# From routing to the first expert: two gathers issued inside the routing's part, levels taken last, four idle transposes in place of 24, x's low parts between two weights' low parts

## The reference, cut to what matters

```python
def hierarchical_moe(u, wg, bg, we, be, w_gate, w_up, w_down):
    xt = u.reshape(t, d)
    g_probs = softmax(xt @ wg + bg);  g_p, g_idx = lax.top_k(g_probs, 1)
    e_in_group = take_along_axis((xt @ we + be).reshape(t, 4, 8), g_idx)
    top_l, top_i = lax.top_k(e_in_group, 2)          # two experts for each token
    gates = g_p * softmax(top_l)
    ...                                              # tokens sorted by expert, in blocks of 128
    x_buf = xt[tok_buf]                              # gather of each block's rows
    def expert_block(args):
        xb, e = args
        return (silu(xb @ w_gate[e]) * (xb @ w_up[e])) @ w_down[e]
    ...                                              # rows scattered back, weighted by the gates
```

## Time and profile before

| | us |
|---|---|
| median of three executions | 2121.59 |
| the profiled execution | 2121.26 |
| its span, first to last instruction | 2119.6 |
| TensorE busy in the span | 2048.2 (97%) |
| VectorE busy | 1605.7 (76%) |
| ScalarE busy | 1361.3 (64%) |
| GpSimd busy | 258.4 (12%) |

### The profile page before, as it was taken

The page is one execution under the profiler, slowest core; times in us unless marked ns, Lnnn a source line. Parts: engine busy times, 40 slices in busy tenths (PEclk is TensorE's granted clock), DMA queues, the critical chain, the costliest instruction groups (busy, mean ns, idle before and its releaser), DMA issues. The chain is left out here.

```text
span 2119.6 us, 30221 instructions
## 1 busy us (share of the span) xinstructions
PE 2048.2 (97%) x10536; PEld 1661.8 (78%) x10536; DVE 1605.7 (76%) x2000; ACT 1361.3 (64%) x1794; POOL 258.4 (12%) x334
## 2 busy tenths in 40 slices
PE   8999998998999999999999989999899999999998
PEld 6888877777788888888877866767688888888885
DVE  4551246777888888888886266887898888888886
ACT  5333426562778787878773256765578888777784
POOL 2000000001111111111102320110111111112210
PEclk9999999999999999999999999999999999999999
DMA  4112222215999999999984020011699999999996
GB/s 138 40 60 90 78 77 74 81 61 196 339 383 388 388 387 384 379 380 380 386 313 144 1 90 11 21 60 50 241 374 380 381 386 386 385 389 384 385 364 253
DMA packets 123491, 513.28 MB, mean 242 GB/s; under 512 B 27373, under 2 KB 28490, under 8 KB 89610
## 3 DMA queue, kind: packets, MB, share of 16 engines
q1 hardware_dynamic: 103674, 474.11, 59.5%
q0 software_dynamic: 18576, 33.86, 4.2%
q10 hardware_dynamic: 1152, 4.19, 0.5%
HBM read 495.05 MB, written 50.86 MB: 258 GB/s over the span
## 5 line engine op out<-in xcount | busy, mean ns | idle before, releaser
L542 DVE TENSOR_TENSOR exp_w_lo<-ring_raw,first_w_hi 128x2048 fp32r<-128x2048 f32 x192 | 439.0, 2288 | 35.2 <-ACT first_w_hi L469 35.2
L542 DVE TENSOR_TENSOR exp_w_lo<-ring_raw,exp_w_hi 128x2048 fp32r<-128x2048 f32 x192 | 439.1, 2289 | 29.8 <-ACT exp_w_hi L469 29.8
L469 ACT ACTIVATE exp_w_hi<-ring_raw 128x2048 fp32r<-128x2048 f32 x192 | 367.8, 1918 | 61.1 <-PE exp_up_out L394 31.1
L469 ACT ACTIVATE first_w_hi<-ring_raw 128x2048 fp32r<-128x2048 f32 x188 | 360.7, 1919 | 60.6 <-PE exp_up_out L394 28.7
L394 PE MATMUL exp_gate_out<-exp_w_lo,exp_x_hi 128*128 128x512 f32 x512 | 200.9, 392 | 0.0
L394 PE MATMUL exp_y_out<-exp_w_lo,exp_hid_hi 128*128 128x512 f32 x512 | 200.2, 391 | 0.0
L394 PE MATMUL exp_up_out<-exp_w_lo,exp_x_hi 128*128 128x512 f32 x512 | 199.2, 389 | 0.0
L339 POOL DMA_INDIRECT y_rows<-exp_y,base_rows_y x63 | 75.6, 1200 | 955.2 <-ACT exp_y L489 955.2
L394 PE MATMUL exp_gate_out<-first_w_hi,exp_x_hi 128*128 128x512 f32 x272 | 109.8, 404 | 3.1 <-issue 2.0
L394 PEld LDWEIGHTS exp_gate_out<-exp_w_lo,exp_x_hi 128*128 128x128 f32 x512 | 96.7, 189 | 19.2 <-issue 0.2
L394 PEld LDWEIGHTS exp_up_out<-exp_w_lo,exp_x_hi 128*128 128x128 f32 x512 | 96.1, 188 | 19.9
(11 more groups left out here) (529 smaller groups left out, 4700.2 us busy)
## 6 DMA issues: line engine op xcount, KB each, us to landing
ring_raw<-in_expert_w_gate_dram SPq DMA_DIRECT2D x128, 1024.0 KB, 10.5
ring_raw<-in_expert_w_up_dram SPq DMA_DIRECT2D x128, 1024.0 KB, 10.9
ring_raw<-in_expert_w_down_dram SPq DMA_DIRECT2D x128, 1024.0 KB, 10.9
l0w_raw<-in_ab_w_in_dram SPq DMA_DIRECT2D x48, 256.0 KB, 2.8
finish_y<-y_rows SPq DMA_DIRECT2D x8, 1024.0 KB, 12.3
ring_raw<-in_swa_w_qkv_dram SPq DMA_DIRECT2D x5, 1024.0 KB, 10.3
ring_raw<-y_rows SPq DMA_DIRECT2D x10, 512.0 KB, 5.1
base_h<-in_x_dram ACTq DMA_DIRECT2D x8, 512.0 KB, 7.0
```

Source lines behind the costliest of these rows:

```text
L469: nc.scalar.activation(split[split_slot(unit)][0][:], raw[raw_slot(unit)][:], ACT.Copy).then_inc(hi_ready, 1)
L542: nc.vector.tensor_tensor(lo[:], raw[raw_slot(unit)][:], hi[:].bitcast(F32), ALU.subtract).then_inc(lo_ready[split_slot(unit)], 1)
```

## The change

Four edits, the same for both layers.

- The gathers of experts 0 and 1 are issued by GpSimd at the end of the routing's stage, ahead of the boundary. They wait for a new semaphore, `tables_made`, and for the stores of `u_rows`.
- `take_levels` stands behind `make_tables`, which raises `tables_made`. Between the entries of tiles a and b there is a drain now.
- TensorE does 4 idle transposes instead of 24 before the first expert's x.
- VectorE makes `x_lo` after low part 8 and before low part 9, no longer after both.

```diff
+    def gather(self, pool, R, u_rows):
+        for e in range(2):
+            pool.indirect_dma_start(self.x_rows[e][:], None, u_rows, bass.IndirectOffsetOnAxis(ap=R.rows_u[:, e:e + 1], axis=0),
+                                    bounds_check=1023, oob_is_err=False).then_inc(self.gathered[e], 16)
...
             def gather(e):
-                if e >= 2:
-                    pool.wait_ge(x_turned_s, e - 1)
+                pool.wait_ge(x_turned_s, e - 1)
...
-            gather(0)
-            gather(1)
             over.gpsimd(pool)
...
-            for k in range(24):
+            for k in range(4):
                 nc.tensor.transpose(x_turned[:, k % 4], c["ident"][:], c["ident"][:])
...
             make_lo((-1, 8))
-            make_lo((-1, 9))
             for half, (made, done) in enumerate(((first_hi, first_lo), (x_hi_s, x_cols_s))):
                 part = slice(4 * half, 4 * half + 4)
                 dve.wait_ge(made, 1)
                 v.tensor_tensor(x_lo[:, part], x_turned[:, part], x_hi[:, part].bitcast(F32), ALU.subtract).then_inc(done, 1)
+            make_lo((-1, 9))
...
                 g.memset(ahead.x_rows[1][:], 0.0)
                 pool.drain()
+                pool.wait_ge(s["tables_made"], 1)
+                pool.wait_ge(stored[0], 48)
+                pool.wait_ge(stored[1], 48)
+                pool.wait_ge(stored[2], 32)
+                ahead.gather(pool, R, u_rows)
...
                 entries_of(a)
+                dve.drain()
+                entries_of(b)
+                dve.drain()
+                make_tables(v, dve, R).then_inc(s["tables_made"], 1)
                 dve.wait_ge(s["counted"], 1)
                 take_levels(v, dve, c, R, counted)
-                entries_of(b)
-                dve.drain()
-                make_tables(v, dve, R)
```

More of the change, by code:

```diff
@@ L994, in layer0 @@
                  "o_turned", "o_hi_made", "o_lo_made", "o_made", "h_made", "h_rooted", "r_rows_made", "r_turned", "r_cols_made", "r_done",
-                 "router_scaled", "last_scaled", "last_gained", "last_rows_scaled", "logits_made", "chosen", "ranked", "marked", "entered", "counted")
+                 "router_scaled", "last_scaled", "last_gained", "last_rows_scaled", "logits_made", "chosen", "ranked", "marked", "entered", "counted", "tables_made")
         s = {n: mem.sem(n) for n in names}
@@ L2319, in layer1 @@
                  "o_hi_made", "o_lo_made", "o_made", "h_made", "h_squared", "h_rooted", "h_scaled", "r_rows_made", "r_turned", "r_cols_made",
-                 "r_made", "router_scaled", "last_gained", "last_rows_scaled", "logits_made", "chosen", "ranked", "marked", "entered", "counted")
+                 "r_made", "router_scaled", "last_gained", "last_rows_scaled", "logits_made", "chosen", "ranked", "marked", "entered", "counted", "tables_made")
         s = {n: mem.sem(n) for n in names}
```

## The result

The changed kernel takes 2132.71 us (median of 5 runs, 2129.64 to 2133.78) against 2121.59 before: a ratio of 1.0049, 95% interval 1.0039 to 1.0059. It is slower by about 11 us, and the time lies above the predicted range. The profiled execution of after took 2129.64 us with a span of 2127.9, 8.3 us more than the span before.

The account below looks back on a forecast made before the run. TensorE was taken to bound each layer's experts from first to last, so time at their start reaches the end. Delay 9.06 minus gain 6.10 gave +3.0 us on 2121.26: 2124.2 us, range 2115.5 to 2128.5.

Parts of the forecast that it names:

- The delay: At the boundary: TensorE's restart (T) comes later behind the gathers, 4.45 us in layer 1, 4.61 in layer 0, together 9.06.
- Tables 0.50 us sooner and levels 0.36 later: End of routing on VectorE: tables made 0.50 us sooner; levels, now last, end the stage 0.36 us later.
- GpSimd's start 0.80 behind the tables: Ahead of the boundary: GpSimd's first gather starts 0.80 us after the tables are made, at 1498.07 in layer 1.
- Second gather 2.75: Ahead of the boundary: the second gather's record lasts 2.75 us in layer 1, as when directly following another gather before.
- the second rival: At the boundary: the second gather is short, 1.02 us; delay 5.6 us together, time 2120.8 us; chance 0.15.
- the third rival: The boundary waits until the gathers have landed: delay 10.1 us per layer, time 2135.4 us, +14.1; chance 0.07.
- The gain: From T, TensorE's restart, through the first expert: work done sooner, 3.04 us in layer 1, 3.06 in layer 0, together 6.1.
- The gate's start: First expert's gate product begins at T + 3.24 instead of T + 7.26, 4.02 us sooner; T is TensorE's restart.
- The clock: TensorE's full clock comes 5.2 us (layer 0: 5.5) after restart; the gate's half-speed stretch costs 0.98 us (layer 0: 1.12).
- the fourth rival: In the gate: clock at half until T + 8.5, costing 2.65 us per layer; gain 1.4, time 2127.6 us; chance 0.09.
- three signs that I had set against the forecast: TensorE's restart within 1 us of its old time, or more than 6 us behind it, or a gate cold throughout its first two units.
- The cold stretch in layer 0 that might vanish: Layer 0's second gate product: eight matmuls took 0.63 instead of 0.39 us; one such stretch more or less, 1.6 us.

Follow-up runs that it names:

- the probe: The changed kernel with a tiny memset, a drain and another memset on GpSimd behind the two gathers, ahead of the boundary: 2128.58 us in one run.
- slow_landing: The changed kernel with layer 1's loads of two weight slots started only when the tables are made, so they move beside the gathers: 2137.96 us in one run.
- the gathers alone: The kernel before with only both gathers moved ahead of the boundary; levels first, 24 idle transposes, x's low parts as before: 2135.25 us, ratio 1.0071.
- one ahead: The changed kernel with only expert 0's gather ahead of the boundary and expert 1's behind it: 2126.70 us, ratio 1.0029.
- the plain copy: The changed kernel with both gathers back behind the boundary and one plain 512 KB GpSimd copy in their place ahead of it: 2132.18 us in one run.
- fill3: The changed kernel with three more idle transposes behind the eight real ones, where TensorE waits for x_lo: 2129.85 us, ratio 1.0046.
- all_but_gathers: The changed kernel with both gathers back behind the boundary, the other edits kept: 2124.42 us, ratio 1.0014.
- abg16: The changed kernel with both gathers back behind the boundary and 16 idle transposes instead of 4: 2121.87 us, ratio 1.0005.

## Why the prediction was wrong

**The step that failed: what the boundary waits for.** I let GpSimd's part end with the second gather's record and gave "waits for the landing" a chance of 0.07, from the 0.30 us of spacing between two gathers, and from a record that ends long before the landing. Neither says anything on a drain: a next DMA, and the probe's first memset too, may start at once, and the drain behind them still waits, as the probe shows. That the boundary waits for the landing is shown by a landing moved alone in `slow_landing`; that it does so by a drain is the likely reason. From the last landing to T are 3.1 to 3.6 us in all eleven cases (after, the gathers alone, one ahead and the probe in both layers, the slow landing, the plain copy in both), where the boundary before took 3.11 and 3.26 us behind VectorE's last instruction.

**The delay, by its terms.** Tables 0.50 us sooner and levels 0.36 later: right to the hundredth in layer 1 (L225 ends 2.57 us behind L195's start, 3.07 before; L214 ends at 1502.63). GpSimd's start 0.80 behind the tables: 0.82 in layer 1 and 0.92 in layer 0. Second gather 2.75: wrong, 0.99 and 1.00, as the second rival had it, and not what decides. Its reason was neither the neighbour nor GpSimd's idle time but VectorE: before, the second gather starts while low part 8 runs, and its record ends 0.87 us behind the end of that; ahead of the boundary no low part runs. The last section has the count. The landing came 1.57 us (layer 1) and 2.60 (layer 0) behind where I had put the record's end, and the boundary took 0.12 and 0.07 longer: 4.45 + 1.57 + 0.12 = 6.14, and 4.61 + 2.60 + 0.07 = 7.28. It is less than the third rival's 10.1 because its 8.4 us to the landing were those of a gather with a record 1.75 us longer and weights moving beside it; ahead of the boundary the second gather took 4.3 and 5.2, and 7.8 with weights beside it again.

**The gain.** The gate's start was right, T + 3.43 and T + 3.56 against 3.24. The clock was not: full at T + 7.5 and T + 7.7, not 5.5 and 5.2. In layer 1 the gate took 7.70 us, 2.00 over its warm length instead of 0.98, and began 0.32 later than forecast: 3.04 - 1.02 - 0.32 = 1.70, as measured. That is nearer the fourth rival's 2.65 than my 0.98, with another reason: the transposes ahead of the gate do count, as `fill3` shows, but I had worked out a wait for `x_lo` behind them and not asked what an idle TensorE does to a clock about to rise. Before, the same wait fell where the clock was full already, and cost nothing. Where such a gap fell ahead of the rise (after, `one_ahead`, `all_but_gathers`) the gate began cold in both layers. The Trainium skill, "TensorE: Matmul & The Clock Gate", section "PE-mode transpose", has transposes not counting for the full clock; by that rule three of them could not have brought it forward, and here they brought it forward by 2.3 and 3.6 us.

**The sum.** Forecast 9.06 - 6.1 = +3.0; measured in the profile 13.4 - 3.75 - 1.2 = +8.5. The third and the fourth rival held together, which I had not priced: each was set against an otherwise true forecast. Of the three signs that I had set against the forecast one came: the restart lies more than 6 us behind its old time (7.78 and 10.64). The cold stretch in layer 0 that might vanish I had named as the forecast's own spread, and it did (it was seven matmuls, not eight). The other 2.6 us between the profile's 8.5 and the medians' 11.1 belong to executions that no trace shows.

**What the change would have needed.** The gathers ahead cost a landing on the path to save a landing off it: before, the gathers landed behind the boundary while the idle turns warmed the clock, and some were needed anyway: with 16 the gate was warm in both layers of `abg16`, with four it was cold in `all_but_gathers`. With the gathers ahead, the restart comes no sooner than landing plus 3.1 us, the least of the eleven. Not tried: a boundary without GpSimd's drain, or the gathers started by another engine.

## What to carry to other kernels

A DMA that GpSimd starts ahead of its drain or of an all-engine barrier puts its whole flight on the path, not its issue: count from the landing. Other engines' DMAs weren't tried. Ask of idle filler what its wait hides before taking it out, and where the clock is about to rise, leave no gap in TensorE's work, even of 0.6 us. And where two doubts are about different terms of one sum, price them together too.

## What was not expected of the hardware

- GpSimd's drain returns 0.1 to 0.2 us behind the landing of the last DMA that GpSimd started (3.75 and 3.77 us behind a memset that ran at once), for gathers; a plain copy holds the boundary as long.
- An idle gap of 0.6 to 0.7 us in TensorE at T + 2.8 put the full clock off from T + 5.2 and T + 4.2 (gap filled) to T + 7.5 and T + 7.7.
- The length of a gather's record depends on what VectorE is doing when it starts. Of the 64 gathers before, the 15 that start while VectorE makes a low part of a weight end 0.87 to 0.91 us behind the end of that low part and last 1.90 to 3.11 us; the other 49 last 0.99 to 1.29. In `plain_ahead` the second gather of layer 0 starts 0.21 us into a low part and takes 2.94 us, and in layer 1 the two start together and it takes 0.99. In layer 0:

```profile
527.75 2.28 DVE L549 TENSOR_TENSOR exp_w_lo<-ring_raw,first_w_hi 128x2048 fp32r<-128x2048 f32 x1
527.96 2.94 POOL L356 DMA_INDIRECT first_x_rows<-u_rows,base_rows_u  x1 [0.30 <-issue]
```

And in layer 1:

```profile
1511.44 2.33 DVE L549 TENSOR_TENSOR exp_w_lo<-ring_raw,first_w_hi 128x2048 fp32r<-128x2048 f32 x1
1511.44 0.99 POOL L356 DMA_INDIRECT first_x_rows<-u_rows,base_rows_u  x1 [0.30 <-issue]
```

That the low part holds the gather back is the plain reading of it; no run moved one against the other on purpose, and why it does isn't shown.
